# Recurrent gate matmuls of a streaming encoder trunk as 64-row tiles, into the scores' and numerators' banks

## The chip, the cores and the metric

The kernel runs on one core of a Trainium2 chip. The metric is the time of one execution on the device in microseconds. The engines are TensorE (PE, with its weight loads PEld), VectorE (DVE), ScalarE (ACT), GpSimd (POOL) and SyncE (SP), which here only issues DMAs.

## The reference, cut to what matters

One layer of a hybrid encoder over 512 new frames and 32 sampled frames, 1024 channels wide: a mixer (a gated recurrence beside a matrix memory with four heads), then a sparse mixture of experts. The change touches the two gates of the recurrence:

```python
xb = x.reshape(Bn, L, LRU_BLOCKS, LRU_BW)            # 16 blocks of 64 channels
r = sigmoid(einsum('blnc,ncd->blnd', xb, w_r).reshape(Bn, L, D_LRU) + b_r)
i = sigmoid(einsum('blnc,ncd->blnd', xb, w_i).reshape(Bn, L, D_LRU) + b_i)
log_a = -LRU_C * r * softplus(-lam)
a = exp(log_a)
u = sqrt(-expm1(2 * log_a)) * (i * x)
h[t] = a[t] * h[t-1] + u[t]
```

`x` is here the output of a causal convolution over the projected frames. Each block of 64 channels is multiplied by its own 64x64 matrix, once for each gate. In the matrix memory (the mLSTM) each head forms scores from queries and keys, numerators from scores and values, and a new state.

## The kernel before, in words

The mixer is run head by head, in one loop over heads 1 to 3 with head 0 ahead of it. A head owns 256 channels of each of five projections, that is ten groups of 128 columns; the recurrence's 256 channels are dealt to the heads in the same way, two tiles of 128 (c = 0 and 1), each of which holds two blocks of 64. Channels lie on partitions, frames (512 + 32, with the conv's rows 548) on the free axis, in two halves of 272 or 274.

**PSUM.** Eight banks: PJ has four, used as two slots of two banks in turn (`pj(u)`, slot u mod 2); MS has two single banks, taken in turn by scores, transposes, denominators and states; NM has two and holds one head's numerators. A use of a PJ slot is signalled by TensorE with `pj_full` and given back with `pj_free`; MS with `ms_full` and `ms_free`; NM is given back with `nm_free` (L1786, the last read of a head's numerators).

**TensorE's order** is written out by hand. In the loop body of head hd: projection groups 0 to 3 of head hd, each followed by one part of head hd-1 (`scores` L1257, `numerators` L1280, `new_state`, `head_squares`), then `second_part` (L1225): groups 4 and 5 (the recurrence's x), the values (groups 6 and 7), the gates of c = 0, groups 8 and 9 (the output gate `og`), and the gates of c = 1. `columns` (L455 is its matmul) multiplies one group in three passes of a split into high and low parts, 48 matmuls of 272 columns.

**The gates** (L1238) are four fp32 matmuls for each c: two gates times two halves of 274 columns. The stationary operand `bd[:, c, m, :]` is a 128x128 tile with the two 64x64 blocks of one gate on its diagonal and zeros elsewhere. Each fp32 matmul is two recorded instructions. Gate m goes to PJ slot m. Its start waits for `conv_done` (the conv of tile c, DVE L1677) and for the slot.

**ScalarE's order** in `second_part` (L892): copy the values out of PSUM (L899, L901), in head 0 also the gate columns (L906, L907), then `gates(0)` (L916: one sigmoid of 128x548 for each gate, L919), `decay(0)` (L928 exp and L929 tanh), a split of weights (L808), `root(0)` (L933), two more L808 with the sigmoids of groups 8 and 9 (L942), then `gates(1)`, `decay(1)`, `root(1)`. Sigmoid, exp with tanh, and sqrt each have a table load ahead of them where the function changes.

**VectorE's order** there: convs of both tiles (L1675, L1677), then `lru(0)` and `lru(1)` (L1691 to L1698: polynomial, products, scans), then `probabilities` of the same head, whose first instruction (L1717) copies the transposed old state out of an MS bank; TensorE's second block of scores (L1271) needs that bank.

**SyncE** loads the weights of each group as a slot comes free; `load_gates` (L494) issues four DMAs into `bd` for the next head, ordered after the last gate matmul of the head before. GpSimd sets constants once at the start, among them `bd` to zero (L661), and all engines wait for their count `NCONST`; later it computes the low parts of split weights (L674).

Of the kernel before, what the change touches and what calls it, by code (L numbers as in the profile page):

```python
# [5 lines left out]
P = 128  # L6
# [8 lines left out]
ds = bass.ds  # L15
# [30 lines left out]
def hawk_mlstm_hmoe_kernel(  # L46
# [56 lines left out]
    RS = NGR // 2  # L103


    PJ_A0, PJ_B0, PJ_LOOP, PJ_HEAD = 2, 6, 16, 14
    PART_B = (4, 5, 6, 7, 10, 11)
    MS_HEAD, MS_PRE = 16, 14
    MS_COLS = 12
    MC = KT // 2  # L110
# [1 line left out]
    with ExitStack() as ctx:  # L112
        def sem(name):
            return ctx.enter_context(nc.semaphore(name))
# [44 lines left out]
        def at(name, *dims, plus=0, mem=plain):  # L159
            n = 1  # L160
            for d in dims:
                n *= d
            v = mem[:, cuts[name] + plus:cuts[name] + plus + n]
            if len(dims) == 1:
                return v
            if len(dims) == 2:
                return v.rearrange("p (a b) -> p a b", a=dims[0])
            return v.rearrange("p (a b c) -> p a b c", a=dims[0], b=dims[1])
# [41 lines left out]
        ident, ones, tri = at("ident", P), at("ones", P), at("tri", P)  # L210
        sel = at("sel", H, P)
        v1, v2, v1t, v2t = at("v1", P), at("v2", P), at("v1t", P), at("v2t", P)
        bd = at("bd", CT, 2, P)
        gcol = at("cols", J, 2 * H)
        cstate = at("cstate", 2, PAD, NCT)
        lst = at("lst", 2, KT)
# [140 lines left out]
        small_out, rows_zeroed, waits_passed = sem("small_out"), sem("rows_zeroed"), sem("waits_passed")  # L357
        ms_full, ms_free, pj_full, pj_free = sem("ms_full"), sem("ms_free"), sem("pj_full"), sem("pj_free")
        nm_full, nm_free = sem("nm_full"), sem("nm_free")
        steps_v, steps_a, steps_p = sem("steps_v"), sem("steps_a"), sem("steps_p")  # L360
        x_root, xn_ready, xh_ready, x_split = sem("x_root"), sem("xn_ready"), sem("xh_ready"), sem("x_split")
        gmix_in, gmix_spread, v_turned = sem("gmix_in"), sem("gmix_spread"), sem("v_turned")
# [31 lines left out]

        rows_of = [P] * JP + [LS]
        CONSTS, LATE_CONSTS = [0], [0]
        NCONST, NLATE = 12, 13
        ORDER = [JP] + list(range(JP))
        HALF = D // 2
        V_HEAD = 62  # L400
# [60 lines left out]
        def _(sp):  # L461
# [32 lines left out]
            def load_gates(hd):  # L494

                for m, w in enumerate((lru_wr, lru_wi)):
                    for half in range(2):
                        blocks = w[0].rearrange("(h c f) p d -> h f p c d", c=CT, f=2)
                        side = slice(64 * half, 64 * half + 64)
                        sp.dma_start(bd[side, :, m, side], blocks[ds(hd, 1), half].rearrange("a p c d -> p (a c) d"))\  # L500
                            .then_inc(bd_in, 16)

            def load_state(hd):
# [25 lines left out]
            def head_loads(hd, ahead):  # L529
                for g in range(RS - 2, NGR):  # L530
                    load_group(hd, g)
                    if g == RS - 1:

                        await_step(sp, pj_full, hd * PJ_HEAD + (PJ_B0 - PJ_HEAD + 10))
                        load_gates(hd)
                    if g == 7:
                        store_state(hd - 1)
                        load_state(hd)
                if ahead:
                    for g in range(RS - 2):  # L540
                        load_group(hd + 1, g)
# [98 lines left out]
        def _(pool):  # L640
# [17 lines left out]
            const(pool.memset(zeros, 0.0))  # L658
            const(pool.memset(at("xpad", P - LS, mem=rounded).bitcast(F32), 0.0))
            const(pool.memset(cin, 0.0))  # L660
            const(pool.memset(bd, 0.0))  # L661
            then(pool.memset(sel, 1.0))

            const(pool.affine_select(out=tri, in_=ones, compare_op=ALU.is_gt, fill=0.0, base=0,
# [125 lines left out]
        def _(act):  # L790
# [101 lines left out]
            def second_part(hd, inputs=(4, 5)):  # L892

                for t in inputs:
                    to_conv(hd, t)
                high_group(hd, 8)
                high_group(hd, 9)
                bank(use_of(hd, 6))
                emptied(act.copy(v[:, 0:JP, :].rearrange("p j n -> p (j n)"), pj(0).rearrange("p a n -> p (a n)")))  # L899
                bank(use_of(hd, 7))  # L900
                emptied(act.copy(v[0:LS, JP, :], pj(1)[0:LS, 0, 0:HD]))  # L901

                if isinstance(hd, int) and hd == 0:
                    for s in range(2):
                        act.wait_ge(ms_full, MS_COLS + s + 1)
                        st.do(act.copy(gcol[:, 0:JP, s * H:(s + 1) * H], MS[:, s, 0:JP * H].rearrange("p (j h) -> p j h", j=JP)))  # L906
                        act.copy(gcol[0:LS, JP, s * H:(s + 1) * H], MS[0:LS, s, JP * H:J * H]).then_inc(gcol_ready, 1)  # L907
                    act.wait_ge(gcol_ready, 2)
                    st.wait()
                    act.sem_inc(ms_free, 2)  # L910
                    act.wait_ge(silu_done, 6)
                else:
                    act.wait_ge(my_done, hd)
                act.wait_ge(cl_ready, 1)

                def gates(c):  # L916
                    for m, name in enumerate(("br", "bi")):
                        bank(part_b(hd) + 4 + 4 * c + m)
                        emptied(act.activation(ri[c][:, m, :].rearrange("p (a n) -> p a n", a=2), pj(m)[:, :, 0:LN_ // 2], ACT.Sigmoid,  # L919
                                               bias=v2t[:, ds(hd * CT + (V2C[name] + c), 1)]))  # L920

                def decay(c):
                    act.wait_ge(pj_free, part_b(hd) + (2 + 4 + 4 * c + 1))
                    if c:

                        act.wait_ge(lru_done, hd * CT + c)
                    scale = cl[:, ds(hd * CT + c, 1)]
                    act.activation(tmp[:, 2, :], ri[c][:, 0, :], ACT.Exp, scale=scale)  # L928
                    act.activation(tmp[:, 3, :], ri[c][:, 0, :], ACT.Tanh, scale=scale).then_inc(decay_ready, 1)  # L929

                def root(c):
                    act.wait_ge(poly_ready, hd * CT + (c + 1))
                    act.activation(tmp[:, 3, :], ri[c][:, 0, :], ACT.Sqrt, scale=-1.0).then_inc(root_ready, 1)  # L933

                gates(0)
                decay(0)
                high_group(hd, 10)
                root(0)
                for m in range(CT):
                    high_group(hd, 11 + m)  # L940
                    bank(part_b(hd) + 6 + m)
                    emptied(act.activation(og[:, m, :].rearrange("p (a n) -> p a n", a=2), pj(m)[:, :, 0:HB], ACT.Sigmoid))  # L942
                gates(1)
                decay(1)
                root(1)

# [212 lines left out]
        def _(pe):  # L1159
# [65 lines left out]
            def second_part(hd):  # L1225
                project(hd, 4)
                project(hd, 5)
                values(hd)
                if isinstance(hd, int) and hd == 0:
                    gate_columns()  # L1230
                await_step(pe, bd_in, hd * 64 + 64)
                for c in range(CT):
                    pe.wait_ge(conv_done, hd * 6 + (2 + 5 + c))
                    for m in range(2):
                        pe.wait_ge(pj_free, part_b(hd) + (4 + 4 * c + m + 1))
                        b = pj(m)
                        for half in range(2):
                            last = pe.matmul(b[:, half, 0:LN_ // 2], bd[:, c, m, :], xc[:, c, half * (LN_ // 2):(half + 1) * (LN_ // 2)],  # L1238
                                             start=True, stop=True)
                        last.then_inc(pj_full, 1)  # L1240
                    if c == 0:
                        project(hd, 8)
                        project(hd, 9)
# [13 lines left out]
            def scores(hd):  # L1257

                pe.wait_ge(c0_in, hd * 32 + 32)
                b = ms_use(0, hd)  # L1260
                for kt in range(CT):
                    for vt in range(CT):
                        last = pe.transpose(b[:, kt * HD + vt * P:kt * HD + (vt + 1) * P], c0[:, vt, kt * P:(kt + 1) * P], ident)
                filled(last)
                pe.wait_ge(silu_done, hd * 4 + 6)
                for j in range(J):
                    b = ms_use(1 + j, hd)
                    quer = slice(P * j, LP) if j < JP else keys_of(j)
                    n = quer.stop - quer.start
                    for ct in range(CT):  # L1270
                        last = pe.matmul(b[0:rows_of[j], 0:n], k[:, ct, keys_of(j)], q[:, ct, quer], start=ct == 0, stop=ct == CT - 1)  # L1271
                    filled(last)
                for m in range(3):
                    b = ms_use(6 + m, hd)
                    for j in range(2 * m, min(2 * m + 2, J)):
                        for ct in range(CT):
                            last = pe.transpose(b[0:rows_of[j], (j % 2) * HD + ct * P:(j % 2) * HD + (ct + 1) * P], k[:, ct, keys_of(j)], ident)
                    filled(last)
# [882 lines left out]
```

## Time and profile before

| | |
|---|---|
| median of 3 runs | 1052.98 us (1052.62 to 1054.36) |
| the profiled execution | 1052.08 us, its span 1050.1 us, mean granted clock 0.963 |
| busy share of the span | PE 91%, PEld 81%, DVE 64%, ACT 52%, POOL 24% |
| chain that ended last | PE 67%, DVE 14%, "issue" 9%, ACT 4%, DMA 2% |
| gate matmuls L1238 | 64 recorded, 16.7 us busy, mean 404 ns of one |
| mixer, heads 0 to 3 | about the first 430 us of the span |

A matmul's recorded duration contains its way through the array, so in a dense stream the distance from start to start is the cost of one, not the duration. A bracket at the end of a row of the timeline is the idle time of that engine just ahead of it, and what released it. "x8" merges eight instructions from the first start to the last end.

### The profile page before, as it was taken

The numbers are of one execution on the slowest core, as the hardware profiler recorded it, in microseconds if no ns is written. First come the engines' busy times: TensorE is split into PE (matmuls) and PEld (weight loads), VectorE is DVE, ScalarE is ACT, GpSimd is POOL, SyncE is SP. The second block draws the span as 40 slices with busy tenths as digits, with TensorE's granted clock in tenths as the row PEclk, the third lists the DMA queues.
The fourth block names the chain that finished last, engine by engine and source line by source line (L and its number), as shares of the span: only waits on it lengthen the run. The fifth ranks groups of instructions, "written<-read, shape, count | busy, mean of one in ns | idle before, by whom it ended". The sixth has DMA issues, their size and how long they took to land.

```text
span 1050.1 us, 16579 instructions
## 1 busy us (share of the span) xinstructions
PE 958.6 (91%) x5923; PEld 847.5 (81%) x5923; DVE 673.9 (64%) x850; ACT 547.5 (52%) x609; POOL 256.0 (24%) x178
## 2 busy tenths in 40 slices
PE   5999899999999998999999999848999999999960
PEld 3999789889978986899999987737788888888740
DVE  5496659767865974621111115389998999989736
ACT  5645525815542572333333224457778788787622
POOL 1013204322320431534334343002011010101022
PEclk9999999999999998999999999969999999999985
DMA  9452122303222220232323368149999999999725
GB/s 288 133 173 66 49 63 62 105 21 90 80 50 65 60 66 15 61 101 80 98 81 81 99 188 309 61 161 330 409 414 412 415 412 415 413 414 413 285 104 212
DMA packets 146596, 193.15 MB, mean 184 GB/s; under 512 B 14471, under 2 KB 91677, under 8 KB 146434
## 3 DMA queue, kind: packets, MB, share of 16 engines
q1 hardware_dynamic: 139000, 165.27, 45.6%
q0 software_dynamic: 4656, 16.21, 4.1%
q10 hardware_dynamic: 2906, 11.23, 2.8%
q8 instruction: 21, 0.34, 0.1%
q14 instruction: 13, 0.11, 0.0%
HBM read 172.91 MB, written 19.77 MB: 183 GB/s over the span
## 4 chain that ended last, share of the span: by engine, by line
PE 67%; DVE 14%; issue 9%; ACT 4%; DMA 2%; SPq 2%; POOL 1%; DVEq 1%; POOLq 0%; ACTq 0%
PE PJ L455 55%; DVE MEM_R L1934 2%; DVE MEM L1677 2%; PE NM L1289 2%; PE PJ L1238 2%; PE MS L1481 1%; DVE MEM L1778 1%; PE MS L1271 1%; PE MS L1309 1%; SPq L599 1%; DMA MEM<-in_x_prompt_dram 1%; PE NM L1429 1%; PE MS L1299 1%; DMA MEM<-expert_rows,MEM 1%; POOL MEM L784 1%
## 5 line engine op out<-in xcount | busy, mean ns | idle before, releaser
L455 PE MATMUL PJ<-MEM_R 128*128 128x272 f32 (+2 forms) x5016 | 805.0, 321 | 10.1 <-DVE MEM_R L2046 3.1
L455 PEld LDWEIGHTS PJ<-MEM_R 128*128 128x128 f32 x5016 | 724.4, 191 | 72.7 <-issue 8.9
L674 POOL TENSOR_TENSOR MEM_R<-RAW,MEM_R 128x1024 fp32r<-128x1024 f32 x72 | 176.2, 2455 | 318.5 <-ACT MEM_R L808 318.5
L1934 DVE TENSOR_TENSOR MEM_R<-CHUNK,MEM_R 128x2048 fp32r<-128x2048 f32 x100 | 224.5, 2284 | 16.1 <-ACT MEM_R L1066 14.8
L1066 ACT CAST MEM_R<-CHUNK 128x2048 fp32r<-128x2048 f32 x100 | 189.3, 1911 | 13.9 <-PE PJ L455 11.3
L808 ACT CAST MEM_R<-RAW 128x1024 fp32r<-128x1024 f32 x81 | 84.3, 1048 | 127.0 <-DMA RAW<-in_w_pb_dram 39.2
L1847 DVE TENSOR_TENSOR MERGED<-PJ,MEM 128x544 f32<-128x544 f32 x16 | 11.6, 725 | 140.9 <-PE PJ L455 131.6
L757 POOL COPY MEM<-MEM 128x1 uint32 (+1 forms) x16 | 18.4, 1149 | 237.7 <-PE MS L1481 237.7
L1677 DVE SCALAR_TENSOR_TENSOR MEM<-MEM 128x548 f32<-128x548 f32 x72 | 58.9, 818 | 8.5 <-DVE MEM L1675 0.9
L1075 ACT CAST MEM_R<-MS 128x1024 fp32r<-128x1024 f32 x17 | 17.3, 1016 | 35.0 <-PE MS L1481 35.0
L865 ACT COPY MEM<-PJ 128x272 f32<-128x272 f32 x24 | 9.0, 377 | 45.9 <-PE PJ L455 45.9
L872 ACT ACTIVATE MEM<-MEM 128x548 f32<-128x548 f32 x16 | 10.6, 663 | 38.1 <-DVE MEM L1677 38.0
L752 POOL DMA_INDIRECT MEM<-t_rows,MEM x18 | 20.6, 1144 | 26.4 <-POOL MEM L757 12.6
L1271 PE MATMUL MS<-MEM 128*128 128x512 f32 (+4 forms) x80 | 22.2, 421 | 4.5 <-DVE MEM L1717 4.4
L885 ACT ACTIVATE MEM<-NM 128x1024 f32<-128x1024 f32 x4 | 4.1, 1024 | 41.9 <-DVE M_Y L1751 41.9
L1691 DVE TENSOR_TENSOR MEM<-MEM 128x548 f32<-128x548 f32 x8 | 5.8, 730 | 30.3 <-ACT MEM L929 30.3
L1082 ACT COPY MEM<-PJ 128x1024 f32<-128x1024 f32 x16 | 16.3, 1017 | 15.7 <-PE PJ L455 15.7
L1271 PEld LDWEIGHTS MS<-MEM 128*128 128x128 f32 (+1 forms) x80 | 12.5, 188 | 14.1 <-DVE MEM L1717 7.7
L1481 PE MATMUL MS<-MEM 128*128 128x128 f32 x136 | 18.5, 281 | 5.2 <-DMA MEM<-t_rows,MEM 5.2
L1481 PEld LDWEIGHTS MS<-MEM 128*128 128x128 f32 x136 | 16.5, 146 | 7.3 <-issue 5.3
L1746 DVE SCALAR_TENSOR_TENSOR MEM<-MS,MEM 128x512 f32<-128x512 f32 x4 | 2.8, 691 | 30.4 <-PE MS L1299 30.4
L2046 DVE TENSOR_TENSOR MEM_R<-MS,MEM_R 128x1024 fp32r<-128x1024 f32 x17 | 20.6, 1214 | 1.5 <-ACT MEM_R L1075 1.5
(305 smaller groups left out, 895.9 us busy)
## 6 DMA issues: line engine op xcount, KB each, us to landing
CHUNK<-in_w_gate_dram SPq DMA_DIRECT2D x34, 1024.0 KB, 8.9
CHUNK<-in_w_up_dram SPq DMA_DIRECT2D x34, 1024.0 KB, 10.5
CHUNK<-in_w_down_dram SPq DMA_DIRECT2D x34, 1024.0 KB, 9.2
RAW<-in_w_in_dram SPq DMA_DIRECT2D x56, 512.0 KB, 3.7
expert_rows<-MEM ACTq DMA_DIRECT2D x16, 512.0 KB, 6.0
expert_rows<-MEM SPq DMA_DIRECT2D x8, 512.0 KB, 5.2
RAW<-in_w_pa_dram SPq DMA_DIRECT2D x8, 512.0 KB, 3.7
RAW<-in_w_pb_dram SPq DMA_DIRECT2D x8, 512.0 KB, 3.7
```

The costliest lines, as they stand in the source:

```text
L455: ins = pe.matmul(out, w(a), x(b), start=first and n == 0, stop=last and n == 2)
L674: tt(lo, raw[slot], hi.bitcast(F32), ALU.subtract).then_inc(lo_done, 1)
L752: pool.indirect_dma_start(out=xg, out_offset=None, in_=t_dram, in_offset=bass.IndirectOffsetOnAxis(ap=index, axis=0)).then_inc(xg_in, 16)
L808: act.copy(hl[slot][0], raw[slot]).then_inc(hi_done, 1)
L1066: act.copy(moe_hl[c][0], moe_raw[c]).then_inc(chunk_hi[c], 1)
L1238: last = pe.matmul(b[:, half, 0:LN_ // 2], bd[:, c, m, :], xc[:, c, half * (LN_ // 2):(half + 1) * (LN_ // 2)], start=True, stop=True)
L1271: last = pe.matmul(b[0:rows_of[j], 0:n], k[:, ct, keys_of(j)], q[:, ct, quer], start=ct == 0, stop=ct == CT - 1)
L1289: last = pe.matmul(NM[:, c, P * j:LP], v[:, j, c * P:(c + 1) * P], dp[:, j, P * j:LP], start=j == 0, stop=j == JP - 1)
L1481: last = pe.transpose(MS[:, half, P * m:P * m + P], xg[:, (4 * half + m) * P:(4 * half + m + 1) * P], ident)
L1677: ins = stt(dst, buf[:, tap:tap + LN_], cw[tap], dst, ALU.mult, ALU.add)
L1934: tt(moe_hl[c][1], moe_raw[c], moe_hl[c][0].bitcast(F32), ALU.subtract).then_inc(chunk_lo[c], 1)
L2046: tt(line(xgT[1]), line(MS), line(xgT[0]).bitcast(F32), ALU.subtract).then_inc(xgT_ready, 1)
```

## The change

The stationary operand becomes 64 rows of one block by 128 columns: both gates' 64x64 matrices side by side. Rows 0 to 63 (first block of the tile) hold r in columns 0 to 63 and i in columns 64 to 127; rows 64 to 127 hold them the other way round. For each half of the frames there is one matmul for the first block into NM and one for the second into MS, so four matmuls for each c, as before, but each over 64 rows. ScalarE reads a gate for each block by itself: four sigmoids of 64x548 for each c in place of two of 128x548. For i the input and the output lie on different halves of the partitions. The gates no longer use PJ; two new semaphores order them: TensorE counts `gates_full`, ScalarE `gates_read`. For c = 0 TensorE waits until NM and MS are free (`nm_free`, `ms_free`), for c = 1 until the four sigmoids of c = 0 are done; `scores` waits until all eight are. The zeroing of `bd` goes.

```diff
-    PJ_A0, PJ_B0, PJ_LOOP, PJ_HEAD = 2, 6, 16, 14
-    PART_B = (4, 5, 6, 7, 10, 11)
+    PJ_A0, PJ_B0, PJ_LOOP, PJ_HEAD = 2, 6, 12, 10
+    PART_B = (4, 5, 6, 7, 8, 9)
...
-        bd = at("bd", CT, 2, P)
+        bd = at("bd", CT, P)
...
-                        side = slice(64 * half, 64 * half + 64)
-                        sp.dma_start(bd[side, :, m, side], blocks[ds(hd, 1), half].rearrange("a p c d -> p (a c) d"))\
+                        side, cols = (slice(64 * s, 64 * s + 64) for s in (half, m ^ half))
+                        sp.dma_start(bd[side, :, cols], blocks[ds(hd, 1), half].rearrange("a p c d -> p (a c) d"))\
...
-                        await_step(sp, pj_full, hd * PJ_HEAD + (PJ_B0 - PJ_HEAD + 10))
+                        await_step(sp, gates_full, hd * 2 * CT)
                         load_gates(hd)
...
-            const(pool.memset(bd, 0.0))
...
                 def gates(c):
-                    for m, name in enumerate(("br", "bi")):
-                        bank(part_b(hd) + 4 + 4 * c + m)
-                        emptied(act.activation(ri[c][:, m, :].rearrange("p (a n) -> p a n", a=2), pj(m)[:, :, 0:LN_ // 2], ACT.Sigmoid,
-                                               bias=v2t[:, ds(hd * CT + (V2C[name] + c), 1)]))
+                    sides = slice(0, 64), slice(64, P)
+                    for n, name in enumerate(("br", "bi")):
+                        for m, b in enumerate((NM, MS)):
+                            act.wait_ge(gates_full, hd * 2 * CT + (2 * c + m + 1))
+                            act.activation(ri[c][sides[m], n, :].rearrange("p (a n) -> p a n", a=2), b[sides[m ^ n], :, 0:LN_ // 2],
+                                           ACT.Sigmoid, bias=v2t[sides[m], ds(hd * CT + (V2C[name] + c), 1)]).then_inc(gates_read, 1)
 
                 def decay(c):
-                    act.wait_ge(pj_free, part_b(hd) + (2 + 4 + 4 * c + 1))
+                    act.wait_ge(gates_read, hd * 4 * CT + (4 * c + 2))
...
                     pe.wait_ge(conv_done, hd * 6 + (2 + 5 + c))
-                    for m in range(2):
-                        pe.wait_ge(pj_free, part_b(hd) + (4 + 4 * c + m + 1))
-                        b = pj(m)
-                        for half in range(2):
-                            last = pe.matmul(b[:, half, 0:LN_ // 2], bd[:, c, m, :], xc[:, c, half * (LN_ // 2):(half + 1) * (LN_ // 2)],
-                                             start=True, stop=True)
-                        last.then_inc(pj_full, 1)
+                    if c:
+                        pe.wait_ge(gates_read, hd * 4 * CT + 4 * c)
+                    else:
+                        pe.wait_ge(nm_free, hd + 1)
+                        pe.wait_ge(ms_free, hd * MS_HEAD + (MS_PRE + 2))
+                    for half in range(2):
+                        for b, side in ((NM, slice(0, 64)), (MS, slice(64, P))):
+                            last = pe.matmul(b[:, half, 0:LN_ // 2], bd[side, c, :],
+                                             xc[side, c, half * (LN_ // 2):(half + 1) * (LN_ // 2)], start=True, stop=True)
+                            if half:
+                                last.then_inc(gates_full, 1)
...
                 pe.wait_ge(c0_in, hd * 32 + 32)
+                pe.wait_ge(gates_read, hd * 4 * CT + 4 * CT)
```

## Rows read from the trace of the kernel before

**Rows 1.** Page, part 1: engine, busy us, share of the span, instructions.
```profile
PE 958.6 (91%) x5923; PEld 847.5 (81%) x5923; DVE 673.9 (64%) x850; ACT 547.5 (52%) x609; POOL 256.0 (24%) x178
```

**Rows 2.** Chain that ended last, head 2: start us, us, what ran.
```profile
290.58 1.92 PE PJ L1238 x8
...
293.37 1.28 ACT L928
...
301.29 3.02 PE MS L1271 x12
```

**Rows 3.** Timeline, PE, head 2: start, us, engine, line, operation, idle before.
```profile
276.06 2.11 PE L1238 MATMUL PJ<-MEM 128*128 128x274 f32 x8 [0.30 <-DVE MEM L1677]
...
278.25 12.33 PE L455 MATMUL PJ<-MEM_R 128*128 128x272 f32 x96
...
290.42 2.07 PE L1238 MATMUL PJ<-MEM 128*128 128x274 f32 x8
...
292.50 6.30 PE L455 MATMUL PJ<-MEM_R 128*128 128x272 f32 x48
...
301.29 3.34 PE L1271 MATMUL MS<-MEM 128*128 128x384 f32 x16 [0.33 <-DVE MEM L1717]
```

**Rows 4.** The same timeline, ACT, head 2.
```profile
277.40 0.72 ACT L919 ACTIVATE MEM<-PJ,MEM 128x548 f32<-128x548 f32 x1 [1.25 <-PE PJ L1238]
...
280.35 0.76 ACT L928 ACTIVATE MEM<-MEM 128x548 f32<-128x548 f32 x1
...
281.01 0.73 ACT L929 ACTIVATE MEM<-MEM 128x548 f32<-128x548 f32 x1
...
290.62 0.62 ACT L942 ACTIVATE MEM<-PJ 128x544 f32<-128x544 f32 x1 [2.14 <-PE PJ L455]
...
292.63 0.72 ACT L919 ACTIVATE MEM<-PJ,MEM 128x548 f32<-128x548 f32 x1 [0.26 <-PE PJ L1238]
...
296.08 1.28 ACT L933 ACT_TABLE_LOAD   x1
...
297.62 0.66 ACT L933 ACTIVATE MEM<-MEM 128x548 f32<-128x548 f32 x1 [0.26 <-DVE MEM L1692]
```

**Rows 5.** The same timeline, DVE, head 2.
```profile
268.80 0.74 DVE L1786 SCALAR_TENSOR_TENSOR M_Y<-NM,MEM 128x512 f32 x1
...
300.57 0.67 DVE L1717 COPY MEM<-MS 128x512 f32<-128x512 f32 x1
```

**Rows 6.** Timeline, PE, head 0.
```profile
88.56 2.12 PE L1238 MATMUL PJ<-MEM 128*128 128x274 f32 x8
...
102.81 2.07 PE L1238 MATMUL PJ<-MEM 128*128 128x274 f32 x8
...
115.50 4.78 PE L1271 MATMUL MS<-MEM 128*128 128x384 f32 x16 [2.28 <-DVE MEM L1717]
```

**Rows 7.** Timeline, ACT, head 0.
```profile
88.74 0.15 ACT L907 COPY MEM<-MS 32x4 f32<-32x4 f32 x1
...
104.91 0.72 ACT L919 ACTIVATE MEM<-PJ,MEM 128x548 f32<-128x548 f32 x1 [0.26 <-PE PJ L1238]
```

**Rows 8.** Timeline, PE, head 3, the last one.
```profile
385.48 6.31 PE L455 MATMUL PJ<-MEM_R 128*128 128x272 f32 x48 [0.91 <-ACT MEM L919]
...
395.41 3.25 PE L1271 MATMUL MS<-MEM 128*128 128x384 f32 x16 [1.47 <-DVE MEM L1717]
```

**Rows 9.** Stretches of head 0: length, five engines' busy us, clock (PEclk), DMA, GB/s.
```profile
118.00:123.00 5.00, 4.11 (x26) 3.30 (x25) 2.77 (x9) 1.04 (x3) 4.32 (x2) 0.82 0.00 0
```

**Rows 10.** Timeline, ACT, start of the kernel.
```profile
10.44 1.06 ACT L801 ACTIVATE MEM<-MEM 128x1024 f32<-128x1024 f32 x1 [1.36 <-DMA MEM<-in_x_prompt_dram]
...
11.62 1.06 ACT L801 ACTIVATE MEM<-MEM 32x1024 f32<-32x1024 f32 x1
...
13.00 1.05 ACT L821 CAST MEM_R<-MS 128x512 fp32r<-128x512 f32 x2
```

**Rows 11.** Timeline, POOL, start of the kernel.
```profile
3.65 0.51 POOL L661 MEMSET MEM<- 128x512 f32 x1
```

More of the change, by code:

```diff
@@ L359, in hawk_mlstm_hmoe_kernel @@
         nm_full, nm_free = sem("nm_full"), sem("nm_free")
+        gates_full, gates_read = sem("gates_full"), sem("gates_read")
         steps_v, steps_a, steps_p = sem("steps_v"), sem("steps_a"), sem("steps_p")
@@ L396, in hawk_mlstm_hmoe_kernel @@
         CONSTS, LATE_CONSTS = [0], [0]
-        NCONST, NLATE = 12, 13
+        NCONST, NLATE = 11, 13
         ORDER = [JP] + list(range(JP))
@@ L940, in second_part @@
                     high_group(hd, 11 + m)
-                    bank(part_b(hd) + 6 + m)
+                    bank(part_b(hd) + 4 + m)
                     emptied(act.activation(og[:, m, :].rearrange("p (a n) -> p a n", a=2), pj(m)[:, :, 0:HB], ACT.Sigmoid))
```

## The prediction

> **What bounds the kernel now.** The first part of the page comes first: TensorE is busy 91% of the span [rows 1], so an edit that takes work from it looks like a gain. That share is an average, so I went on to the chain of waits around the gates. In head 2 it goes from the gate matmuls of c = 1 to ScalarE's exp of the decay, and comes back to TensorE only at the second block of scores, L1271 [rows 2]. Between them lie `decay(1)`, `lru(1)` and VectorE's copy of the old state. The timelines say the same: TensorE stands 0.33 us ahead of that block and is released by the copy L1717, which starts at 300.57 as soon as VectorE is through with `lru(1)` [rows 3, 5]. At the other end, the gates of c = 0 wait 0.30 us for the conv on VectorE [rows 3]. So a head period has two places at which TensorE is not the one that is late: the entry to gates 0 (VectorE) and the entry to L1271 (ScalarE, then VectorE). Time saved on TensorE between the two does not shorten the head by itself; what counts is **when ScalarE has ended the sigmoids of c = 1**. In head 0 the idle time ahead of L1271 is already 2.28 us, in head 3 it is 1.47 us [rows 6, 8].
>
> Everything behind L1271 up to the next conv is left as it is, and so are the experts. A shift at L1271 is therefore carried to the end; I take it over one to one.
>
> **The change part by part.**
>
> *Gate matmuls.* Eight recorded instructions for each c, 292.50 - 290.42 = 2.08 us, so 0.26 us each [rows 3]. After it there are again eight, on 64 rows each. No row here shows two halves of the array at work on different matmuls, so I bound the block. Above: no overlap, 2.08 us. Below: full overlap, 1.04 us; weight loads forbid much less, since a dense stream of load and matmul runs at 12.33/96 = 0.128 us a pair, eight pairs 1.03 us [rows 3]. In between: a matmul is two passes over the same rows, issued one behind the other, and only the next matmul has the other rows. If the order is kept, pass 2 of one runs beside pass 1 of the next: 5 slots in place of 8, 1.30 us. I take 1.30, because it follows from the written order, and keep 1.04 and 2.08 as ends.
> A rule of the Trainium skill says more: the page TensorE: Matmul & The Clock Gate, Part 3, gives a pack of tiles the time of one matmul and about 4 ns for each further tile. By it the block would take 1.04 us and the sum below would be 0.6 us instead of 1.6. The page TensorEngine Tiling (Array Packing), Key Properties, speaks against the change: a change of tiling mode drains the engine. It gives no price, and no run here shows one.
>
> *The order between them.* Groups 8 and 9 take 290.42 - 278.25 = 12.17 us [rows 3] in every case. The start of gates 0 (276.06) is set by the conv and stays. So gates 1 start at 276.06 + 12.17 + block: 289.27 (full), 289.53 (mine), 290.31 (none). Today 290.42.
>
> *ScalarE.* A sigmoid starts 277.40 - 276.06 - 4 x 0.26 = 0.30 us behind the pass that it needs [rows 3, 4]. The new first sigmoid needs NM's second half. That is complete after 1.04 us in the full and in my case (slot 4 of 5), after 6 x 0.26 = 1.56 us with none. Then four run in a row. Instructions of this width start 281.01 - 280.35 = 0.66 us apart, and the last lasts 0.72 [rows 4]: 3 x 0.66 + 0.72 = 2.70 us. Half the partitions give nothing back: the square of 32x1024 takes 1.06 us, as that of 128x1024 [rows 10]. Sigmoids of gates 1 end, in head 2, at
> full 289.27 + 1.04 + 0.30 + 2.70 = 293.31; mine 293.57; none 290.31 + 1.56 + 0.30 + 2.70 = 294.87; today 292.63 + 0.72 = 293.35 [rows 4].
> The shift is **-0.04, +0.22 or +1.52 us** for each of heads 1 to 3. What TensorE gains, the two added sigmoids eat.
>
> *Covers of this.* The sigmoids of gates 0 end 1.03 us later (277.40 + 2.70 = 280.10; today 280.35 less a table load of 1.28, 279.07) [rows 4]. Ahead of the last `og` sigmoid ScalarE idles 2.14 us [rows 4]; the projection it waits for now ends 0.89 earlier, so 0.2 us of slack is left. If that goes, each further 0.1 us is paid in full. `lru(0)` ends 1.03 later too, but the table load of the decay does not wait for it: the one at 296.08 ran 1.5 us ahead of an activation that was itself held by VectorE until 297.62 [rows 4]. Nothing there.
>
> *Head 0* has another start. The gates must wait until ScalarE has copied the gate columns out of MS: L907 ends at 88.74 + 0.15 = 88.89, with 0.2 for the signals (an estimate from the 0.30 above) 89.1, for 88.56 today [rows 6, 7]. Gates 1 then start at 89.1 + block + 12.17 = 102.31, 102.57 or 103.35 (today 102.81), and the sigmoids end at 106.35, 106.61 or 107.91; today 104.91 + 0.72 = 105.63 [rows 7]. Shift **+0.72, +0.98 or +2.28 us**.
>
> *The freed slots and the added waits.* Groups 8 and 9 and the next head's group 0 no longer wait for gate sigmoids: 0.1 us each today, contained above. NM must be free before gates 0: its last read starts 268.80 and takes 0.74, 6.5 us of cover [rows 5]. `scores` waits for all eight sigmoids: they end near 293.6 and `scores` follows a 6 us projection from 290.8, 3 us of cover. SyncE's four `bd` DMAs keep size and place in its queue; their wait names the same matmul. All nothing.
>
> *The start.* The memset of 0.51 us goes from POOL [rows 11]; at most -0.5. I take 0: the first copies of x on ScalarE (13.00) follow its squares of the last frames without idle time [rows 10], and those wait for x, not for a constant.
>
> Base sum: 0.98 + 3 x 0.22 = **+1.6 us** (full overlap 0.72 - 0.12 = +0.6; none 2.28 + 4.56 = +6.8).
>
> *The clock.* TensorE now stands longer ahead of L1271. In head 2 group 0 starts at 289.53 + 1.30 = 290.83 for 292.50, so idle is 0.33 + 1.67 + 0.22 = 2.2 us. In head 3 it is 1.47, plus the 0.91 that goes in front of L455 [rows 8], plus 1.7 and 0.2: 4.2 us. What such a pause does shows in head 0: after 2.28 us of idle the granted clock of the next stretch is 0.82 of full, a part of it at 1.2 GHz [rows 9], and the block of 16 takes 4.78 us, where it takes 3.34 behind 0.33 us and 3.25 behind 1.47 us [rows 3, 6, 8]. The price of a fall is 4.78 - 3.34 = 1.44 us, on the path. Heads 1 and 2 come to just about the idle time at which head 0 fell, head 3 to far more. I take two of the three: 2.9 us. Ends: none, and all three (4.3); below that, even head 0's own fall may land elsewhere (-1.4).
>
> **Sum:** 1.6 + 2.9 = +4.5 us. On the profiled execution 1052.08 gives 1056.6; the median lies 0.90 above that execution, so 1052.98 + 4.5 = **1057.5 us**.
>
> **Rivals.**
> *The clock stays up* (chance 0.27). The passes overlap wholly or in part and no further fall comes: +0.6 to +1.6, 1053.6 to 1054.6, no change that shows. For it: 1.47 us did nothing in head 3. Against: 2.28 us did in head 0, and the pauses now reach it.
> *The tiles don't overlap* (0.20). The change does not do what it says, each matmul is as long as before and the sigmoids are doubled: +6.8, and with the idle time at 0.33 + 0.1 + 1.5 = 1.9 us none to two falls, 1059.8 to 1062.7. For it: no overlap shows in any row. Against: different rows, different banks.
> *A faster kernel* (0.07). Its place is the four sigmoids: were one on 64 partitions half as long, they would take 3 x 0.33 + 0.36 = 1.35 us in place of 2.70, so each head would end 1.35 us earlier: 4 x -1.35 + 0.6 = -4.8, 1048.2. It decides from a sigmoid of under about 0.55 us on. Against it stand the two squares of equal time [rows 10].
>
> **How the numbers follow.** A measurement of this kernel can tell about 0.2%, 2.1 us, from no change. My forecast, one to three falls on the base sum (+3 to +6, 1056 to 1059), has 0.46. Slower by more than that: 0.46 + 0.20 = 0.66. Within: 0.27. Faster: 0.07. The range runs from full overlap with a fall less than today, 0.6 - 1.4 = -0.8, 1052.2, to no overlap with two falls, 6.8 + 2.9, 1062.7. It holds forecast and first two rivals and leaves out the faster one and a little more.
>
> **What the profile would show.** Right: the gate block on PE 1.3 us long; four L919 for each c, 0.72 each, 0.66 apart; ScalarE's decay of c = 1 within 0.3 us of its old place behind gates 0; idle ahead of L1271 of 2 us and more in each head; a clock below 1.0 there. Wrong: a block near 2 us (no overlap); L919 well under 0.7 us; L1271 starting earlier behind gates 0 than the 301.29 - 276.06 = 25.2 us of today; or a conv that ends earlier, so that gates 0 move, which I hold fixed.

## The result, and the profile after

The change made the kernel a little slower: 1056.74 us median (1052.20 to 1061.63, 19 runs) against 1052.90 us (1048.84 to 1056.56, 19 runs), a ratio of 1.0044, 95% interval 1.003 to 1.0058. The profiled execution of after took 1052.90 us with a span of 1051.0 us; that is at the low end of its runs, so the profile shows less of the loss than the median does.

Part 1 of the page of after, beside [rows 1]:

```profile
PE 951.2 (90%) x5923; PEld 841.3 (80%) x5923; DVE 677.1 (64%) x850; ACT 558.6 (53%) x625; POOL 256.0 (24%) x177
```

TensorE has 7.4 us less to do, ScalarE went from 547.5 to 558.6 us, and the span is 0.9 us longer. The timeline of TensorE in head 2 of after, as [rows 3]:

```profile
277.10 0.49 PE L1243 MATMUL NM<-MEM 64*128 64x274 f32 x1 [0.36 <-DVE MEM L1684]
277.11 0.49 PE L1243 MATMUL MS<-MEM 64*128 64x274 f32 x1
277.43 0.39 PE L1243 MATMUL NM<-MEM 64*128 64x274 f32 x1
277.44 0.39 PE L1243 MATMUL MS<-MEM 64*128 64x274 f32 x1
277.66 0.39 PE L1243 MATMUL NM<-MEM 64*128 64x274 f32 x1
...
278.23 12.32 PE L456 MATMUL PJ<-MEM_R 128*128 128x272 f32 x96
290.48 0.49 PE L1243 MATMUL NM<-MEM 64*128 64x274 f32 x1
...
302.88 3.34 PE L1278 MATMUL MS<-MEM 128*128 128x384 f32 x16 [2.82 <-DVE MEM L1724]
```

Each NM matmul (rows 0 to 63) has an MS matmul (rows 64 to 127) 0.01 us behind it, and four such pairs make the block: 278.23 - 277.10 = 1.13 us, where it took 2.19. The two halves of the array run side by side. (About 0.4 us of the 2.19 was no work of TensorE but a wait for a PJ slot: in the run banks below the full matmuls take 1.75 us.) But the pause ahead of the second block of scores went from 0.33 to 2.82 us. From the first gate matmul to that block it is 302.88 - 277.10 = **25.78 us, before 25.23**. ScalarE and VectorE say why, beside [rows 4, 5]:

```profile
278.42 0.71 ACT L921 ACTIVATE MEM<-NM,MEM 64x548 f32<-64x548 f32 x1 [1.29 <-PE MS L1243]
279.16 0.71 ACT L921 ACTIVATE MEM<-MS,MEM 64x548 f32<-64x548 f32 x1
279.90 0.72 ACT L921 ACTIVATE MEM<-NM,MEM 64x548 f32<-64x548 f32 x1
280.65 0.71 ACT L921 ACTIVATE MEM<-MS,MEM 64x548 f32<-64x548 f32 x1
281.37 1.28 ACT L930 ACT_TABLE_LOAD   x1
...
294.02 0.71 ACT L921 ACTIVATE MEM<-MS,MEM 64x548 f32<-64x548 f32 x1
294.95 1.28 ACT L930 ACT_TABLE_LOAD   x1 [0.22 <-DVE LRU_Y L1705]
```

```profile
285.51 2.93 DVE L1700 TENSOR_TENSOR MEM<-MEM 128x548 f32<-128x548 f32 x1
...
291.43 3.18 DVE L1704 TENSOR_TENSOR_SCAN LRU_Y<-MEM 128x512 f32 x1
294.54 0.25 DVE L1705 TENSOR_TENSOR_SCAN LRU_Y<-MEM 128x32 f32 x1
...
302.16 0.67 DVE L1724 COPY MEM<-MS 128x512 f32<-128x512 f32 x1
```

The four sigmoids start 0.74 us apart and last 0.71, so they run for 2.94 us, to 281.36. The exp, `root(0)`, and with them `lru(0)`, are pushed back; VectorE's product L1700 and scan L1704 last about 3 us each beside GpSimd's splits (for c = 1, without a split, the same product takes 0.72 us), and `lru(0)` ends at 294.79. Only then, 0.22 us behind the last sigmoid, does the table load of `decay(1)` start: 294.95. Before, it came 17.31 us behind the first gate matmul, now 17.85.

Heads 0 and 3 of after, and two stretches (columns as in [rows 9]), beside [rows 6, 8, 9]:

```profile
86.18 0.71 PE L1257 MATMUL MS<-MEM 4*128 4x4 f32 x10
87.35 0.47 PE L1243 MATMUL NM<-MEM 64*128 64x274 f32 x1 [0.46 <-ACTq L910]
...
114.93 5.67 PE L1278 MATMUL MS<-MEM 128*128 128x384 f32 x16 [4.63 <-DVE MEM L1724]
```

```profile
396.11 4.94 PE L1278 MATMUL MS<-MEM 128*128 128x384 f32 x16 [4.84 <-DVE MEM L1724]
```

```profile
115.00:121.00 6.00, 5.77 (x18) 3.93 (x19) 1.87 (x5) 3.46 (x6) 4.00 (x3) 0.57 0.00 0
303.00:309.00 6.00, 5.19 (x31) 3.74 (x32) 3.70 (x10) 0.80 (x1) 4.08 (x2) 1.00 0.00 0
```

In head 0 the gates start 1.17 us behind the first gate column's transpose, before 0.64, and reach the scores 27.58 us later, before 26.94. Behind pauses of 4.6 to 4.8 us the clock was down in heads 0 (0.57 of full in the first of the two stretches) and 3 (the block took 4.94 us); behind 2.8 us in heads 1 and 2 it was not (3.34 us, 1.00 in the second stretch).

The whole path, first gate column to the end of the mixer's chain (L455 at 435.78 before, L456 at 436.44 after), by stretches, after less before:

| stretch | before | after | change |
|---|---|---|---|
| head 0: gate columns to gates 0 | 0.64 | 1.17 | +0.53 |
| gates 0 to second scores, heads 0, 1, 2, 3 | 26.94, 25.22, 25.23, 27.24 | 27.58, 25.78, 25.78, 27.81 | +0.64, +0.56, +0.55, +0.57 |
| second scores to next gates 0, heads 0, 1, 2 | 68.43, 66.91, 66.88 | 69.41, 66.98, 65.42 | +0.98, +0.07, -1.46 |
| second scores of head 3 to the mixing stage | 40.37 | 40.33 | -0.04 |

The first two lines, **+2.85 us**, are the change's own path. Nothing that it edits lies in the other two; what moved there in these two profiles was the clock: the block of scores of head 0 ran longer at a low clock, and a fall behind the small matmuls in head 2, which cost 1.5 us before (L455 x48 in 7.79 us), did not come. Ahead of all this after was 1.7 us early at the gate columns (86.18 for 87.92), and behind it 0.2 us late. Gates 0 of head 0 start between 86.8 and 88.9 us in the thirteen profiles of this study, in no order that follows the kernels (87.35 in after, 88.54 in serial and 86.83 in swap, which have the same code up to there), so I count the 1.7 as scatter.

### The profile page after: what moved, and what is told of

It reads as the page before. It is cut to its first block, busy times and chain, and to the rows that moved or that the text cites. A ratio compares the mean times of both kernels' runs of the same rounds, so it can differ in the third digit from the quotient of the medians.

```text
span 1051.0 us, 16609 instructions
## 1 busy us (share of the span) xinstructions
PE 951.2 (90%) x5923; PEld 841.3 (80%) x5923; DVE 677.1 (64%) x850; ACT 558.6 (53%) x625; POOL 256.0 (24%) x177
## 4 chain that ended last, share of the span: by engine, by line
PE 61%; DVE 18%; issue 11%; ACT 5%; DMA 2%; DVEq 1%; POOL 1%; POOLq 0%; ACTq 0%; SPq 0%
PE PJ L456 50%; DVE MEM_R L1941 3%; DVE MEM L1684 2%; PE NM L1296 2%; PE MS L1278 2%; DVE MEM L1702 1%; DVE MEM L1785 1%; PE MS L1316 1%; PE MS L1488 1%; DVE MEM L1700 1%; DMA MEM<-in_x_prompt_dram 1%; ACT MEM L921 1%; PE NM L1436 1%; PE MS L1306 1%; ACT L930 1%
## 5 line engine op out<-in xcount | busy, mean ns | idle before, releaser
L456 PE MATMUL PJ<-MEM_R 128*128 128x272 f32 (+2 forms) x5016 | 803.5, 321 | 9.0 <-DVE MEM_R L2053 3.1
L456 PEld LDWEIGHTS PJ<-MEM_R 128*128 128x128 f32 x5016 | 722.6, 191 | 71.8 <-issue 8.7
L1278 PE MATMUL MS<-MEM 128*128 128x512 f32 (+4 forms) x80 | 24.7, 457 | 15.2 <-DVE MEM L1724 15.1
L1084 ACT COPY MEM<-PJ 128x1024 f32<-128x1024 f32 x16 | 16.3, 1017 | 16.0 <-PE PJ L456 16.0
L899 ACT COPY MEM<-PJ 128x1024 f32<-128x1024 f32 x4 | 4.1, 1015 | 33.2 <-PE PJ L456 33.2
```

What stands on the lines that cost most here:

```text
L456: ins = pe.matmul(out, w(a), x(b), start=first and n == 0, stop=last and n == 2)
```

## The experiments

Theory 1: the two added sigmoids for each c delay `lru(0)` and `decay(1)`, and TensorE's gain lies beside the path. Theory 2: the banks and the waits for them cost. Theory 3: the clock behind the longer pauses costs. All ratios are to before, measured beside each run. "The path" is from the first gate matmul of head 2 to the second block of scores: 25.23 before, 25.78 after.

**halfsig: the sigmoids cut in two, nothing else (on before).**

```diff
-                        emptied(act.activation(ri[c][:, m, :]..., pj(m)[:, :, 0:LN_ // 2], ACT.Sigmoid, bias=v2t[:, ...]))
+                        for side in (slice(0, 64), slice(64, P)):
+                            ins = act.activation(ri[c][side, m, :]..., pj(m)[side, :, 0:LN_ // 2], ACT.Sigmoid, bias=v2t[side, ...])
+                        emptied(ins)
```

> The kernel before with one part of the change: each gate sigmoid is cut in two of 64 partitions, matmuls, slots and banks stay. Theory 1 (the doubled sigmoids delay lru(0) and with it the decay of c = 1): about 0.74 us from sigmoid to sigmoid, the table load of the first decay 1.3 us later, and from the first gate matmul of c = 0 to the second block of scores 25.8 us in heads 1 to 3, where it was 25.2; with the median 0.2 to 0.3% above before. Theory 2 (the cost is that of the banks and the waits for them): 25.2 us, a ratio of 1.000. Theory 3 (the cost is the clock behind longer pauses alone): pauses hardly grow here, to 0.9 us in heads 1 and 2, so 1.000 too.

Measured: ratio 1.0028 (1.0007 to 1.005). TensorE in head 2:

```profile
276.83 2.11 PE L1240 MATMUL PJ<-MEM 128*128 128x274 f32 x8 [0.27 <-DVE MEM L1679]
279.74 12.33 PE L455 MATMUL PJ<-MEM_R 128*128 128x272 f32 x96 [0.79 <-ACT MEM L920]
...
294.71 6.30 PE L455 MATMUL PJ<-MEM_R 128*128 128x272 f32 x48 [0.73 <-ACT MEM L920]
...
304.00 3.34 PE L1273 MATMUL MS<-MEM 128*128 128x384 f32 x16 [0.83 <-DVE MEM L1719]
```

The path is 27.17 us, more than theory 1 had: with half sigmoids in the projections' slots, group 8 waits 0.79 us and the next head's first group 0.73 us until a slot is read. So the freed slots are worth something once the sigmoids are four, and halfsig is no clean copy of after's sigmoids. Theories 2 and 3 fall as sole causes: there are no new banks here and the pauses in heads 1 and 2 are 0.83 us.

Four such paths are 7.8 us longer than before's, and the ratio gives only about 3 us. The profile shows a part of the difference: from the second scores to the next gates 0 heads 1 and 2 take 65.37 and 65.34 us, before 66.91 and 66.88, because the clock did not fall behind the small matmuls there. A longer path is not passed on one to one while the clock moves with it.

**banks: the banks and waits alone (on after).** Block-diagonal `bd` of 128 rows and its memset are back.

```diff
-                    for half in range(2):
-                        for b, side in ((NM, slice(0, 64)), (MS, slice(64, P))):
+                    for m, b in enumerate((NM, MS)):
+                        for half in range(2):
                             last = pe.matmul(b[:, half, 0:LN_ // 2], bd[:, c, m, :], xc[:, c, ...], start=True, stop=True)
...
+                    for m, (name, b) in enumerate((("br", NM), ("bi", MS))):
+                        act.wait_ge(gates_full, hd * 2 * CT + (2 * c + m + 1))
+                        act.activation(ri[c][:, m, :]..., b[:, :, 0:LN_ // 2], ACT.Sigmoid, ...).then_inc(gates_read, 2)
```

> The other part alone: gates of c = 0 and 1 go to NM (r) and MS (i) under the new waits, but as four full 128-row block-diagonal matmuls and with two sigmoids of 128 partitions. Theory 1: gates to L1271 in 25.1 to 25.2 us in heads 1 to 3, in head 0 a start 0.5 us later behind the gate columns' copies; ratio within 0.1% of before. Theory 2 (banks and waits cost): 25.8 us and a ratio of 1.002 to 1.004. Theory 3: a pause of some 0.5 us at L1271, no fall, 1.000.

Measured: ratio 1.0009 (0.9987 to 1.0031). Its scores in head 2 start 297.98 - 273.16 = 24.82 us behind the gates:

```profile
273.16 1.19 PE L1242 MATMUL NM<-MEM 128*128 128x274 f32 x4 [0.40 <-DVE MEM L1682]
274.19 1.09 PE L1242 MATMUL MS<-MEM 128*128 128x274 f32 x4
274.91 12.42 PE L456 MATMUL PJ<-MEM_R 128*128 128x272 f32 x96
...
297.98 3.34 PE L1276 MATMUL MS<-MEM 128*128 128x384 f32 x16 [0.63 <-DVE MEM L1722]
```

The banks take 0.4 us off the path. Theory 2 falls. The block of full matmuls takes 274.91 - 273.16 = 1.75 us here for 2.19 before, since group 8 no longer waits until the gates' slot is read. So of the 1.06 us that the block became shorter with the change, 0.44 come from the banks and 0.62 from the tiles. Against this kernel the tiles with their four sigmoids add 25.78 - 24.82 = 0.96 us to the path of a head.

**serial: the tiles' order turned (on after).**

```diff
-                    for half in range(2):
-                        for b, side in ((NM, slice(0, 64)), (MS, slice(64, P))):
+                    for b, side in ((NM, slice(0, 64)), (MS, slice(64, P))):
+                        for half in range(2):
```

> The kernel after with the tiles' order turned: both halves of the frames for the first 64 rows, then both for the other 64, so that neighbours share their rows and run one after the other; the gate block should take 1.9 to 2.1 us for 1.1. Theory 1 (TensorE's gain is not on the path): the sigmoids that read MS start 0.3 us later, gates to L1278 take 26.1 us for 25.8, pauses ahead of L1278 shrink from 2.8 to about 1.5 us in heads 1 and 2: within 0.1% of the kernel after, ratio to before 1.003 to 1.005. Rival (the overlap of tiles is worth its 1 us a block): 8 us more than after, ratio 1.012.

Measured: ratio 1.0032 (1.0011 to 1.0053). TensorE in head 2, and the scores of head 1 with the stretch around them:

```profile
279.31 0.49 PE L1243 MATMUL NM<-MEM 64*128 64x274 f32 x1 [0.37 <-DVE MEM L1684]
279.33 0.49 PE L1243 MATMUL MS<-MEM 64*128 64x274 f32 x1
279.64 0.39 PE L1243 MATMUL NM<-MEM 64*128 64x274 f32 x1
279.66 0.39 PE L1243 MATMUL MS<-MEM 64*128 64x274 f32 x1
...
280.45 12.34 PE L456 MATMUL PJ<-MEM_R 128*128 128x272 f32 x96
```

```profile
211.39 5.84 PE L1278 MATMUL MS<-MEM 128*128 128x384 f32 x16 [2.83 <-DVE MEM L1724]
```

```profile
211.00:217.00 6.00, 5.61 (x16) 3.82 (x16) 1.91 (x4) 1.32 (x4) 4.57 (x2) 0.50 0.00 0
```

The experiment did not do what it was made for: issued as NM, NM, MS, MS, the matmuls still ran as pairs 0.02 us apart and the block took 1.14 us. It left the worth of the overlap open (banks, with full matmuls in the same banks, comes nearest to showing it) and is in effect a second look at after (path 25.80). As such it shows the scatter of the clock: behind the same pause of 2.83 us its block of scores in head 1 took 5.84 us at a granted clock of 0.50 (1.2 GHz), after's 3.34 at 1.00.

**filler: matmuls without use in the pause (on after).**

```diff
                 for j in range(J):
+                    if j == 1:
+                        for _ in range(3):
+                            pe.matmul(NM[:, 0, :], k[:, 0, keys_of(0)], q[:, 0, 0:LP], start=True, stop=True)
```

> The kernel after with three matmuls without use (fp32, 128x512, 2.6 us in all) into NM in the pause ahead of the second block of scores of each head. Theory 3 (the part of the loss beyond the 0.55 us a head is the clock): pauses fall from 2.8 to about 0.2 us in heads 1 and 2 and from 4.7 to 2.1 in heads 0 and 3, the block L1278 takes 3.3 to 4.8 us everywhere, the median falls by 1 to 2 us against the kernel after, to a ratio of about 1.0025. If the clock has no part: the same 1.0044 or a little above, where the filler holds up the scores.

Measured: ratio 1.0029 (1.0008 to 1.0049), against 1.0044 for after and 1.0032 for serial; the intervals overlap. The pauses are 2.06, 0.24, 0.23 and 2.30 us; the block took 3.34 us in heads 0 to 2, and 4.94 us still in head 3, here heads 0 and 3:

```profile
116.00 3.34 PE L1281 MATMUL MS<-MEM 128*128 128x384 f32 x16 [2.06 <-DVE MEM L1727]
```

```profile
394.87 4.94 PE L1281 MATMUL MS<-MEM 128*128 128x384 f32 x16 [2.30 <-DVE MEM L1727]
```

The mean granted clock of its runs was 0.964, after's 0.960, so the filler did what it was made for. The time doesn't follow clearly: the ratio is 0.0015 under after's, about 1.6 us, but its median is 4.3 us above that of before beside it (1056.51 and 1052.17), no less than after's 3.8. Whether theory 3 has a part in the time, and how large, stays open.

**early: another order (on after).** ScalarE: split of group 10, gates 0, decay 0, root 0, first output gate, gates 1, decay 1, root 1, second output gate; the wait of the last head's first mix is set one `pj_free` lower and the full one put ahead of `mix(0, 1)`.

```diff
+                high_group(hd, 10)
                 gates(0)
                 decay(0)
-                high_group(hd, 10)
                 root(0)
-                for m in range(CT):
-                    high_group(hd, 11 + m)
-                    bank(part_b(hd) + 4 + m)
-                    emptied(act.activation(og[:, m, :]...))
+                out_gate(0)
                 gates(1)
                 decay(1)
                 root(1)
+                out_gate(1)
...
-                    if c == 0:
-                        project(hd, 8)
-                        project(hd, 9)
+                    project(hd, 8 + c)
```

> The kernel after with another order: ScalarE splits the next head's first group ahead of gates 0 (in its pause there), TensorE multiplies gates 1 between groups 8 and 9, and ScalarE puts gates 1, decay 1 and root 1 ahead of the second output gate. If the chain gates 0, lru(0), decay 1, lru(1) is what holds back the second block of scores (theory 1), this takes it off the path: lru(0) no longer collides with three GpSimd splits and lru(1) ends before TensorE comes. From gates 0 to L1278 about 23 us for 25.8, pause there near zero, 8 to 11 us less than after, a ratio to before of 0.991 to 0.994. If TensorE's banks or the clock set the time, the ratio stays at 1.003.

Measured: ratio 1.0012 (0.9993 to 1.003), against 1.0044: faster than after, but far less than expected. Path 24.87 us:

```profile
300.39 3.34 PE L1279 MATMUL MS<-MEM 128*128 128x384 f32 x16 [1.88 <-DVE MEM L1726]
```

```profile
297.45 2.30 DVE L1707 TENSOR_TENSOR_SCAN LRU_Y<-MEM 128x32 f32 x1
```

The pause is still 1.88 us. The last 32 columns of `lru(1)` lasted 2.30 us, because ScalarE's split behind `root(1)` had started GpSimd's part of it just then (296.46 to 299.67). And not all of the path's gain reaches the end: the four paths together take 101.3 us for after's 107.0, but from the end of head 3's scores to the mixing stage it is 41.5 us, in before 37.1, with a granted clock of 0.50 from 400 to 404 and from 428 to 432 us and a wait for VectorE of 2.12 us where before has 0.61.

**early_banks: the same order with the banks alone** (the diff above on banks).

> The same order with the kernel of the banks alone (full 128-row matmuls, two sigmoids). Theory 1: here TensorE is the bound once the chain is short; gates to L1271 24.2 us for 24.8 with the banks alone, a ratio of 0.995 to 0.998. The tiles' 1 us a block should now show as the difference from the run before: 4 heads by 2 blocks by 1.0 us minus what is left of pauses, some 5 us.

Measured: 1040.90 us, **ratio 0.9891 (0.9868 to 0.9914)**, faster than both kernels.

```profile
266.42 1.19 PE L1245 MATMUL NM<-MEM 128*128 128x274 f32 x4 [0.36 <-DVE MEM L1684]
...
276.04 12.42 PE L456 MATMUL PJ<-MEM_R 128*128 128x272 f32 x96
...
288.74 4.95 PE L1277 MATMUL MS<-MEM 128*128 128x512 f32 x20
```

```profile
355.81 1.19 PE L1245 MATMUL NM<-MEM 128*128 128x274 f32 x4 [0.36 <-DVE MEM L1684]
```

```profile
285.99 2.36 DVE L1705 TENSOR_TENSOR_SCAN LRU_Y<-MEM 128x32 f32 x1
288.94 0.69 DVE L1724 COPY MEM<-MS 128x512 f32<-128x512 f32 x1 [0.59 <-PE MS L1269]
```

The scan is blocked here too (2.36 us), but `lru(1)` ends at 288.35, ahead of the copy's transposes: all 20 score instructions run as one piece, with no pause. A head takes 355.81 - 266.42 = 89.39 us, where it took 92.11; of these 2.7 us, 1.5 are a fall of the clock behind the small matmuls that came in head 2 of before and not here. From gates 0 to the end of the scores the four heads take 27.59, 27.28, 27.27 and 27.20 us, before 31.72, 28.56, 28.57 and 30.49: 10.0 us less, of which 1.4 are head 0's low clock, so 8.6 are the order's and the banks' own. That 10.0 is also the difference of the spans (1050.1 and 1040.0) is chance: an earlier start gives 1.3 and the falls missing between the heads 4.4, and behind head 3's scores 5.6 are lost, 4.2 of them before the mixing stage, to the clock and the same wait as in early. The tiles did not show their gain here: full matmuls gave the faster kernel.

**high10: the move of one split alone (on after).**

```diff
+                high_group(hd, 10)
                 gates(0)
                 decay(0)
-                high_group(hd, 10)
```

> The kernel after with one move alone: the split of the next head's first group ahead of gates 0. Theory 1: lru(0) starts no earlier, but collides with two splits on GpSimd and not three and ends 2 us earlier; then the sigmoids of c = 1, not lru(0), set decay 1: gates to L1278 25.5 us for 25.8, within 0.1% of after. A rival: lru(0) was the whole chain, and the gain is 2 us a head, 8 us in all.

Measured: ratio 1.0032 (1.0015 to 1.005), path 302.53 - 276.94 = 25.59 us, 0.2 below after, as theory 1 had it: with `lru(0)` out of the way the sigmoids of c = 1 are next, 0.2 us earlier.

```profile
302.53 3.34 PE L1281 MATMUL MS<-MEM 128*128 128x384 f32 x16 [2.62 <-DVE MEM L1727]
```

**swap: the two waits of decay 1 in the other order (on after).**

> The kernel after with the two waits of decay 1 in the other order, lru(0) first and the sigmoids second. If the table load is held by the earlier one of two waits, it changes nothing, since lru(0) is now the earlier wait: start 0.2 us behind the last sigmoid, chain 25.78. If it is held by every wait but the last, the present order would already let it run ahead of lru(0), which the trace denies. Either way 25.7 to 25.8 us a head. A chain of 25.5 would say that the wait for lru(0) as second in line is what cost the 0.2 us.

Measured, in one profiled execution: 302.17 - 276.38 = 25.79 us. No change, so the order of the waits is not the lever.

**early_h12: early with tiles, the last split ahead of decay 1**, and **early_banks_h12**, the same with the banks.

```diff
                 gates(1)
+                high_group(hd, 12)
                 decay(1)
```

> The tiles in the early order, with the last split (third group of the next head) moved from behind root 1 to ahead of decay 1, so that its GpSimd part no longer meets the last scan of lru(1), which stood blocked for 2.3 us. Theory 1: gates to L1278 24.87 - 2.3 + 1.04 = 23.6 us, which is 0.6 us above TensorE's own 23.0; 1.3 us a head less than the early order with tiles: a ratio of 0.993 to 0.998, if pauses of 0.6 us bring no fall of the clock. If the pause at this block were not what makes the tiles late, the ratio stays at 1.001.

> The same move on the fastest kernel so far (full matmuls, two sigmoids, early order). There VectorE was through with lru(1) 0.6 us ahead of TensorE, so nothing should come: 0.989 within 0.15%. It also measures the early order with the banks once more: a ratio of 0.987 to 0.991 if that gain is real.

Measured: early_h12 1045.32 us, ratio 0.9939 (0.9915 to 0.9962); path 293.14 - 269.24 = 23.90 us, pause 0.95 us:

```profile
293.14 3.34 PE L1281 MATMUL MS<-MEM 128*128 128x384 f32 x16 [0.95 <-DVE MEM L1728]
```

early_banks_h12 1043.13 us, ratio 0.9922 (0.9901 to 0.9944), above the 0.989 that was expected, with an interval that overlaps early_banks' own: the gain of this order is 0.8 to 1.1%. One instruction moved took 1 us a head off the path with tiles, as theory 1 has it. The time of early_h12 fell by more than these 4 us, 0.0073 or 7.7; early's profile has a fall of the clock between the heads three times, that of early_h12 never (65.5 us from the second scores to the next gates 0 in each head, in early 67.0 or more). A head takes 358.61 - 269.24 = 89.37 us with tiles and 358.92 - 269.57 = 89.35 us with full matmuls: the 0.6 us that the tiles save in each block buy nothing even in this order, since the four sigmoids keep a pause of 0.95 us that the full matmuls don't have.

**mid_banks: early_banks with the first split where it was.**

> The early order with the banks, but the split of the next head's first group stays behind decay 0, so only the gates of c = 1 move. If the place of gates 1 is what gives the gain, lru(0) collides with GpSimd again and ends near 14 us behind gates 0, lru(1) near 22, just as TensorE comes: 0.989 to 0.992. If the gain comes from taking lru(0) out of the splits' way, most of it is lost: 0.996 or more.

Measured: ratio 0.9953 (0.9934 to 0.9973), between the two forecasts; path 295.33 - 270.75 = 24.58 us, pause 0.36. Each of the two moves gives a part: from gates 0 to the end of the scores, the move of gates 1 takes 0.24 us off head 2 and 2.3 off head 3 (banks against mid_banks), the move of the split another 0.65 and 0.6 (mid_banks against early_banks).

## Why the prediction was right

It said 1057.5 us, slower with a chance of 0.66, and 1056.74 was measured (+3.8 us of medians, for +4.5 forecast). Direction and mechanism hold; the terms don't all, and that the sum came within 1 us is luck: a base that was too small and a clock term that was too large made up for each other.

- **What bounds the head.** Right. The entry to gates 0 stayed with VectorE's conv (0.36 us of idle), and TensorE's gain turned into a pause: 2.82 us, forecast 2.2. banks shows that the loss isn't the banks' (path 0.4 us shorter), so it lies with the tiles and their four sigmoids.
- **The gate block.** Mis-sized: 1.30 us forecast "because it follows from the written order", 1.13 measured. The step that failed is that the order of issue decides which matmuls pair. serial shows that it doesn't. The price of a pass was wrong too: I divided 2.08 us by eight, but those 2.08 hold a wait for the slot, which I had put at 0.1 us; banks takes 1.65 for the block at gates 1, so the wait is 0.43. The Trainium skill's page TensorE: Matmul & The Clock Gate, Part 3, was nearer: a pack takes the time of one matmul, and the trace agrees within a pair (starts 0.01 us apart, pairs 0.23 apart). A cost for the change of mode, which the Trainium skill's page TensorEngine Tiling (Array Packing), Key Properties, names, is at most about 0.1 us on the way in (277.43 - 277.10 = 0.33 for a step of 0.23) and 0.1 on the way out. It did not matter: the forecasts for 1.04 and 1.30 differ by 1 us in all.
- **The sigmoids.** The term was mis-sized: 2.70 us for four, 0.66 apart, taken from exp and tanh out of SBUF; measured 2.94, 0.74 apart, hardly overlapped. Half the partitions did give nothing back.
- **"Nothing there" for lru(0).** This cover failed. I read from `root` that a table load runs ahead of its activation's wait; `root` has one wait, `decay(1)` two, and its table load started only behind `lru(0)`. Why it waited is not shown; swap shows only that the order of the two waits isn't the reason. So `lru(0)`, 1.2 us later behind gates 0 than before, set the path: +0.55 us a head for a forecast +0.22. high10, where `lru(0)` ends early, has +0.36: of the 0.33 that I missed, 0.19 are `lru(0)` and 0.14 the sigmoids less the block. The base sum was +2.85 instead of +1.6.
- **Head 0's start.** +0.53 for +0.54 forecast, right.
- **The clock.** The sum had +2.9 for two more falls. In the profiled execution the stretches that only the clock moves add up to -0.45. What the medians leave for it is 3.8 - 2.85, about 1 us, and by the ratio (4.6 us) about 1.8. So this term was too large by 1 to 2 us and made up for the base's 1.2. That the rest is the clock is likely but not shown: after's 19 executions have a mean granted clock of 0.960, before's 0.962 to 0.963, and after's fastest has 0.964 (1052.20 us), its slowest 0.957 (1061.63); filler raised the clock to 0.964, and its time fell by 1.6 us at most. What I took for a cost of 1.44 us a fall is partly paid back: in head 3 the block of scores took 1.7 us longer, but the stretch to the mixing stage as a whole was not longer (-0.04), since the fall that had come later before, in the numerators (5.51 us, now 4.48), did not come then.
- **Rivals.** "The tiles don't overlap" fell. "A faster kernel" fell with its price (0.71 us for a half sigmoid). "The clock stays up" was the case of heads 1 and 2 of the profiled execution.

## What to carry to other kernels

Ask of a saved microsecond on the busiest engine where it next waits: here two stages behind, for a chain of sigmoids, a scan and a copy on two other engines, so halving a matmul block at the price of two more instructions on ScalarE lost time. The same look at the chain found the gain: moving gates 1 and one split within the order, with the matmuls left full in the new banks, gave 0.989, and 0.992 with one more split moved. Splitting an instruction over partitions doubled its cost on ScalarE (0.71 us for 64 partitions, 0.72 for 128).

## What the runs showed of the hardware

- Matmuls on rows 0 to 63 and 64 to 127 run side by side in fp32, into different banks, and pair up even when issued as two and two: starts 0.02 us apart [serial], the block 1.14 us in both orders.
- Pauses of TensorE and its clock are not tied one to one. Behind pauses of 2.6 to 2.85 us in heads 1 and 2 the block of scores was slow in 3 of 8 cases (after, serial, high10, swap), behind 1.91 us or less in none, behind 4.66 to 4.88 us in head 3 in 4 of 4. In heads 0 and 3 it was slow behind 2.08 us [mid_banks], 2.28 [before] and 2.30 [filler], but not behind 2.50 and 2.66 [banks]. In head 3 of after a fall in the scores stood in place of one in the numerators before.
- The small VectorE scan of 32 columns lasted 0.26 us by itself and 2.3 us beside a GpSimd split.
